# Second layer of a four-stage network: the modulation's gathers on ScalarE's DMA queue, two tiles scaled ahead of the modulation

## What is computed

```python
shift, scale, gate = adaln(c, mod_w[i], mod_b[i])             # rows of 1024
shift_c, scale_c, gate_c = adaln(c_ctx, mod_w[i], mod_b[i])
u_lat = rms_norm(h_lat, norm_g[i]) * (1.0 + scale) + shift      # 4 tiles of 128 tokens
u_ctx = rms_norm(h_ctx, norm_g[i]) * (1.0 + scale_c) + shift_c  # 2 tiles
...
q, k, v, z = jnp.split(u @ w_in, 4, axis=-1)                  # w_in: 1024 x 8192
```

## Time and profile before

| | before |
|---|---|
| median of 3 runs | 3225.17 us (3225.07 to 3231.73) |
| profiled execution | 3222.18 us, span 3220.4 us |
| mean granted TensorE clock | 0.971 |
| TensorE busy | 3026.0 us, 94% of the span |
| VectorE busy | 1522.1 us, 47% |
| ScalarE busy | 812.0 us, 25% |
| GpSimd busy | 444.0 us, 14% |

### The profile page before, as it was taken

The page is one execution under the profiler, slowest core; times in us unless marked ns, Lnnn a source line. Parts: engine busy times, 40 slices in busy tenths (PEclk is TensorE's granted clock), DMA queues, the critical chain, the costliest instruction groups (busy, mean ns, idle before and its releaser), DMA issues. The chain is left out here.

```text
span 3220.4 us, 37627 instructions
## 1 busy us (share of the span) xinstructions
PE 3026.0 (94%) x14339; PEld 1959.2 (61%) x14339; DVE 1522.1 (47%) x3450; ACT 812.0 (25%) x2062; POOL 444.0 (14%) x745
## 2 busy tenths in 40 slices
PE   5999999999999997999999999979999999589699
PEld 2445555555555544887878786547888885244374
DVE  2344554554554435556556654334565563331431
ACT  1013333333333322123232332212122221120141
POOL 1221231231230010202011110000011110010000
PEclk8999999999999998999999999989999999799799
DMA  7330010010014004211212123042111100311001
GB/s 236 144 118 27 27 53 26 27 53 27 27 53 131 1 0 144 69 48 53 73 47 73 40 72 138 1 115 53 27 27 39 41 27 1 124 53 56 26 1 53
DMA packets 137899, 189.06 MB, mean 59 GB/s; under 512 B 21836, under 2 KB 90476, under 8 KB 135668
## 3 DMA queue, kind: packets, MB, share of 16 engines
q1 hardware_dynamic: 136520, 186.57, 18.2%
q10 hardware_dynamic: 1200, 0.09, 0.0%
HBM read 176.97 MB, written 9.67 MB: 58 GB/s over the span
## 5 line engine op out<-in xcount | busy, mean ns | idle before, releaser
L488 PE MATMUL a_psP<-a_w,a_uT 128*128 128x512 f32 x1536 | 700.1, 601 | 5.8 <-DMA a_w<-a_w_in 5.8
L488 PEld LDWEIGHTS a_psP<-a_w,a_uT 128*128 128x128 f32 x1536 | 280.5, 192 | 323.2 <-issue 323.2
L737 DVE TENSOR_REDUCE a_small<-a_psS 128x1 f32<-128x768 f32 (+1 forms) x192 | 140.8, 775 | 402.0 <-PE a_psS L516 402.0
L1460 PE MATMUL b_psP<-b_w,b_uT 128*128 128x256 f32 x768 | 183.8, 382 | 0.8 <-DVE b_raw L1743 0.3
L643 ACT ACTIVATE a_e<-a_psS,a_small 128x768 f32<-128x768 f32 (+1 forms) x192 | 143.8, 753 | 139.1 <-DVE a_small L737 138.7
L1460 PEld LDWEIGHTS b_psP<-b_w,b_uT 128*128 128x128 f32 x768 | 141.7, 190 | 23.7 <-issue 3.8
L1780 DVE TENSOR_REDUCE b_small<-b_psS 128x2 f32<-128x512 f32 x64 | 44.3, 691 | 213.0 <-PE b_psS L1517 213.0
L538 PEld LDWEIGHTS a_psO<-a_v,a_pT 128*128 128x128 f32 x896 | 115.1, 192 | 45.9 <-issue 45.9
L650 ACT COPY a_pT<-a_psS 128x768 f32<-128x768 f32 (+1 forms) x96 | 63.0, 656 | 311.4 <-PE a_psS L525 311.4
L1617 ACT ACTIVATE b_e<-b_psS,b_small 128x512 f32<-128x512 f32 x128 | 86.7, 682 | 192.0 <-DVE b_small L1793 190.1
L1624 ACT COPY b_e<-b_psS 128x512 f32<-128x512 f32 x128 | 71.8, 587 | 228.5 <-PE b_psS L1527 147.2
(11 more groups left out here) (479 smaller groups left out, 5368.1 us busy)
## 6 DMA issues: line engine op xcount, KB each, us to landing
a_w<-a_w_in SPq DMA_DIRECT2D x16, 2048.0 KB, 8.7
b_w<-b_w_in SPq DMA_DIRECT2D x48, 512.0 KB, 3.8
a_yT<-mod_w SPq DMA_DIRECT2D x8, 1536.0 KB, 8.5
a_yT<-mod_w SPq DMA_DIRECT2D x8, 1024.0 KB, 18.2
b_yT<-b_w_in SPq DMA_DIRECT2D x16, 512.0 KB, 3.7
f_place<-bias_table SPq DMA_DIRECT2D x64, 128.0 KB
f_place<-a_w_in SPq DMA_DIRECT2D x16, 512.0 KB, 6.5
d_w<-a_w_in SPq DMA_DIRECT2D x16, 512.0 KB, 6.9
```

The source lines that it names most:

```text
L488: ins = nc.tensor.matmul(s.psP[:, x % 2, :], s.uT[:, a, t * P:(t + 1) * P], w[:, a, :], start=(a == 0), stop=(a == KD - 1))
L737: nc.vector.tensor_reduce(self.nm[i % 2][:, k:k + 1], self.score_banks(k, keys), AX_X, ALU.max, negate=True).then_inc(self.mx, 1)
L1460: ins = nc.tensor.matmul(out, lhsT, rhs, start=(a == 0), stop=(a == 3))
```

## The change

The five gathers move from SP's list to the front of ScalarE's (`mod_load`, in place of `mod_sync`). In VectorE's list `scaled` of tiles 0 and 1 goes ahead of `modulation`.

```diff
-    def mod_sync(self, sp):
+    def mod_load(self, act):
         for r in range(2):
-            sp.dma_start(self.s.mod[:, r, 1, :], self.e_rows[r, 0:D].rearrange("(a p) -> p a", p=P),
+            act.dma_start(self.s.mod[:, r, 1, :], self.e_rows[r, 0:D].rearrange("(a p) -> p a", p=P),
                          allow_slow_non_contiguous=True).then_inc(self.mod_in, 16)
-            sp.dma_start(self.scale[:, r, :], self.e_rows[r, D:2 * D].rearrange("(a p) -> p a", p=P),
+            act.dma_start(self.scale[:, r, :], self.e_rows[r, D:2 * D].rearrange("(a p) -> p a", p=P),
                          allow_slow_non_contiguous=True).then_inc(self.mod_in, 16)
-        sp.dma_start(self.gcol, self.g.rearrange("(a p) -> p a", p=P),
+        act.dma_start(self.gcol, self.g.rearrange("(a p) -> p a", p=P),
                      allow_slow_non_contiguous=True).then_inc(self.mod_in, 16)
...
             for t in range(2):
                 norm.rows_sync(sp, t)
-            norm.mod_sync(sp)
             for n in range(4):
                 mixer.load(sp, 0, n)
...
-            norm.modulation(dve)
             for t in range(2):
                 norm.scaled(dve, t)
+            norm.modulation(dve)
...
         def _(act):
+            norm.mod_load(act)
             for t in range(2):
                 norm.squares(act, t)
```

## The result

The changed kernel takes 3233.34 us (median of 8 runs, 3229.45 to 3237.73) against 3224.76 us for the kernel before (8 runs, 3221.28 to 3231.73). The ratio is 1.003, with a 95% interval of 1.0018 to 1.0042. It is slower by 8.6 us; 3235.5 was predicted. Its profiled execution has a span of 3227.6 us.

What follows compares the result with a forecast made beforehand. TensorE bounds the second layer's body (594.10 of 600 us busy), so a shift at its head moves the end. +11.3 - 1.0 = +10.3 us, on a median of 3225.17, gave 3235.5 us; range 3223.0 to 3238.5.

Steps and rivals of the forecast that it cites:

- one for one: Second layer's head: one gather element passes per SP packet, so modulation fills near 1269 us, evacuation 11.3 us later; chance 0.55.
- as before: Rival at the second layer's head: gathers land by 1255 us or so, evacuation 1.4 us earlier, 3223.8 us; chance 0.18.
- two elements for one: Rival at the second layer's head: two gather elements per SP packet, modulation full at 1260.7, +2.7 us, 3227.9 us; chance 0.16.
- The head start: Start of the second layer: about 30 gather elements per engine pass while only the identity is moving, for 0.39 us.
- The sum's first term: Second layer's head: the first evacuation begins at 1269.6 instead of 1258.33, 11.3 us later.
- ScalarE's issues: Second layer's head: five issues on ScalarE, the third perhaps stalling 2.73 us, making tile 0's Square 0.9 us later.
- The rival in which this stall is added to the end: Second layer's head: fifth issue near 1265, squares held past the modulation, another +1.5 us, 3237 us; chance 0.08.
- What comes back: After the second layer's late evacuation: 0 to 3 us of the loss is regained, taken as 1 us.
- the spared fall: First projection, second layer: shorter TensorE idle may spare the clock's second fall, to 0.52, worth up to 1.5 us.
- The first: Second layer's head: rows 2 to 5 already landed, so VectorE's four 0.44 us waits for GpSimd disappear.
- The order of the scaling: Second layer's head: scaling before modulation gains at most 1.4 us, or 2.3 us without the ScalarE stall, if modulation lands unchanged.
- whatever moves the evacuation moves the rest: Second layer's head, evacuation to 1266.77 us: VectorE's work runs almost back to back, so a shift carries through.

Runs made afterwards that it cites:

- e3: The changed kernel, but SP waits for all five gathers before issuing rows 2 to 5 and the constants; 3227.01 us (1 run).
- e5: The changed kernel, but SP waits for all five gathers before issuing the weights and all that follows; 3222.93 us (1 run).
- e8: The kernel before, with scaling ahead of the modulation and only the norm_g gather moved to ScalarE's queue; 3221.66 us (1 run).
- e7: The changed kernel with three whole-row transfers on ScalarE's queue, one transpose and small copies replacing the five gathers; 3219.66 us (11 runs), ratio 0.9993 to the kernel before.
- e4: The changed kernel, but ScalarE squares tiles 0 and 1 before issuing the gathers; 3236.21 us (1 run).
- e1: The kernel before with only VectorE's order changed, scaling of tiles 0 and 1 ahead of modulation, gathers on SP; 3223.09 us (10 runs), ratio 1.000.
- e6: The kernel before with scaling first and three whole-row transfers on SP's queue, one transpose and small copies replacing the gathers; 3224.16 us (1 run).
- e2: The kernel before with only the five gathers moved to ScalarE's queue, modulation still ahead of scaling; 3237.44 us (1 run).

## Why the prediction was right

*The exchange of packets.* The step "one for one" is what the queues of the changed kernel show from 4.15 us on, at two sizes of SP's packets. It was a better choice than its source: at the opening, 557 packets of SP's passed beside 254 elements, 2.2 for one. There SP's packets weighed 7.3 KB (4.09 MB / 557); why the gather got less there is open. The landing does not hang on the exact ratio, though. One element for one packet, or fewer, leaves gathers over when SP's queue is empty, and then they land with the last of the work. e3, e5 and e8 show that it is the packets beside the gathers, and e7 that it is the gathers' number of packets, and not ScalarE's queue as such, that make them late. The two rivals in which the modulation lands earlier fall: L1030 came at 21.62 us, not at 8 to 10 (as before) or at 13.7 (two elements for one; by the prediction's own terms, 1252.3 + 8.0, that is 1260.3 and not 1260.7, so 13.3, which changes nothing).

*When the last gather lands.* I let it land with the last of the DMA work, 22.3 us after the identity's issue; it was 21.6. The head start was mis-sized: by 4.15 us 100 elements per engine had passed beside 20 packets of SP's, against the 30 of the prediction, and after that 3603 gather packets met 3457 of SP's. So the gathers outlasted SP's queue by only 146 packets, 9 per engine; the prediction had 49 to spare (320 against 30 + 241). e4 shows that a smaller head start alters nothing; by these counts, one larger by more than 9 per engine would have let the last gather land ahead of SP's last packets. The sum's first term was 11.3 us and measured 10.6.

*ScalarE's issues.* I expected the third to stall, for 2.73 us in all, with the first Square 0.9 us later. The fourth and the fifth stalled, and the Square was 3.4 us later. e4 shows the cost: none while the modulation is later still. The rival in which this stall is added to the end needed a fifth issue near 1265 us. In the changed kernel it went out at 1250.60 and ended 7.34 us after the identity's issue, and the transposes of tile 1 were done almost 8 us ahead of L1030.

*What comes back.* I took 1 us out of 0 to 3. It is 1.6 us: the head is 10.6 us late at the evacuation, 10.4 at product 6 and 9.0 at the marker. The difference is in product 6, whose 12 matmuls take 2.86 us after, at a granted clock of 1.00, and 4.35 us before, where the clock fell to 0.52. Of the two sources that I named it is the second one, the spared fall, worth 1.5 us as its upper bound said; TensorE had been idle for 1.19 us ahead of product 6, against 3.24 before. The first shows nothing at TensorE: three of VectorE's four waits for GpSimd are gone, but tile 2's transposes follow product 6 without a gap. These start at 24.00 us before and 32.92 after, 8.9 us apart. TensorE's timeline before:

```profile
1270.96 1.04 PE L1067 MATMUL b_psS<-f_identity,b_yT 128*128 128x128 f32 x8
```

And after:

```profile
1279.27 1.04 PE L1067 MATMUL b_psS<-f_identity,b_yT 128*128 128x128 f32 x8
```

So the term "11.3 - 1.0" came out as 10.6 - 1.6 = 9.0 us. The medians differ by 8.6 us, and the interval of the ratio, 5.8 to 13.5 us, holds both this and the 9.0 of the layer. With 3224.76 us as the base, the kernel before's median over all 8 runs, the predicted step of 10.3 us is 1.3 us more than the layer shows.

*The order of the scaling.* I put its most at 1.4 to 2.3 us with the modulation as before. e1 shows 2.0 us at the evacuation, of which 0.5 us is left at tile 2's transposes. I had not foreseen that the rest would be lost at TensorE's lower clock; the argument "whatever moves the evacuation moves the rest" holds for the loss of 9 us, but not for a gain of 2.

The Trainium skill's sentence in "DMA: Bandwidth & Descriptors", section "Issuing engines are not separate DMA queues", that all issuers' transfers interleave on the same engines, agrees with the rows here (1340 against 1337 packets); its remark that a second issuer only saves issue time is not what this kernel shows, since the order of service changed and cost 9 us. As to the same page's packet of up to 64 descriptors (section "SWDGE vs HWDGE vs iDMA"), the equal counts beside weights and rows, 1337 to 1340 and 650 to 649, do not fit turns of many elements against single rows. The 557 gather packets beside 79 of SP's before that could be such turns; nothing here tells.

## What to carry to other kernels

A second DMA queue is not a fast lane. Here two full queues shared each engine packet for packet, beside packets of SP's of 1 to 4 KB, and beside larger ones at the opening the gather got even less. So a transfer of many tiny packets that somebody waits for does best ahead of the bulk on the same queue, or as a few whole rows, which landed early on either queue (e6, e7). Before moving a transfer, count its packets per engine against those that the other queue will hold at that time; and after a gain at the head of a stage look at whether TensorE's granted clock gives part of it away again.

## What I had not expected

The issue of a gather on a queue that drains slowly beside a full one held the issuing engine for as long as 8.05 us (e4), with all its arithmetic behind it; it was harmless only because everything there waited for the same data.

The same 12 matmuls of product 6 took 2.86 us in e7 and 5.49 us in e1, though both wait for the same VectorE instruction and start within 0.2 us of each other. TensorE had been idle 2.29 us before them in e7 and 3.42 us in e1. Where the granted clock is 0.50 it runs at 1.2 GHz, half of its upper level. The other traces fall in line. Product 6 took 2.86 us where TensorE had been idle for 1.02 to 2.29 us before it (the changed kernel, e3, e4, e7), and 4.35 to 5.49 us, at the lower clock for part or all of it, where it had been idle for 3.05 to 3.42 us (before, e1, e2, e5, e6, e8). Whether the idle time is the cause was not tried, and neither level of this product moved the late marker by itself: e6 and e7 differ there by 0.1 us.
